# Attention units issued in twos on TensorE, with scores of the two partition halves alternating between two PSUM banks

## The reference, cut to what matters

```
logits = q @ k.T * scale + bias_or_mask      # 128 x nk, nk = 128 for query block 0, 256 for block 1
p      = exp(logits - max(logits)); den = sum(p)
out    = (p @ v) / den * factor              # 128 x 64 (128 x 128 in the differential and memory attention)
```

## Time and profile before

| | |
|---|---|
| median of 3 runs | 1821.94 us |
| lowest, highest | 1797.82, 4195.58 us |
| the profiled execution | 1794.75 us |
| its span, first to last instruction | 1792.9 us |
| PE busy | 94% |
| DVE busy | 60% |
| ACT busy | 47% |
| share of PE in the chain that ended last | 90% |
| mean granted TensorE clock | 0.952 |

### The profile page before, as it was taken

One profiled execution on the slowest core, in us unless ns is written; L12 is line 12 of the kernel. 1 busy time (PEld: TensorE's weight loads), 2 busy tenths in 40 slices (PEclk: granted clock), 3 DMA queues, 4 the chain that ended last, 5 costly groups with the idle time before them and its releaser, 6 DMA issues.

```text
span 1792.9 us, 25005 instructions
## 1 busy us (share of the span) xinstructions
PE 1680.8 (94%) x10388; PEld 1508.4 (84%) x10388; DVE 1069.4 (60%) x1551; ACT 848.0 (47%) x1215; POOL 12.8 (1%) x19
## 2 busy tenths in 40 slices
PE   7969898899998999997979999999999999999998
PEld 7867787799978998785767899879998877789996
DVE  4547566588846554576747655546554775755553
ACT  4446543566535443453336544444443554654441
POOL 0000000000000000000000000000000000000000
PEclk9969999899998999997589999999999999999999
DMA  7723255455553555452034445545555432425553
GB/s 269 274 102 124 78 204 188 142 177 187 188 189 140 188 179 196 166 185 97 1 115 144 159 176 184 188 171 181 188 188 188 165 141 95 159 100 179 177 188 115
DMA packets 42928, 290.21 MB, mean 162 GB/s; under 512 B 5000, under 2 KB 5150, under 8 KB 9920
## 3 DMA queue, kind: packets, MB, share of 16 engines
q1 hardware_dynamic: 38272, 271.93, 42.8%
q0 software_dynamic: 4544, 16.69, 2.8%
HBM read 287.51 MB, written 8.55 MB: 165 GB/s over the span
## 4 chain that ended last, share of the span: by engine, by line
PE 90%; DVE 5%; ACT 2%; DVEq 2%; DMA 1%; issue 1%; SPq 0%; POOL 0%; POOLq 0%; ACTq 0%; PEldq 0%
PE bank L443 26%; PE bank L444 25%; PE bank L445 25%; PE bank L449 8%; PE bank L705 2%; PE bank L1295 2%; DVEq L1990 2%; DVE low L411 1%; DMA raw<-stream_dram 1%; PE bank L595 1%; ACT high L400 0%; PE bank L456 0%; DVE u L924 0%; DVE h L1000 0%; DVE u L648 0%
## 5 line engine op out<-in xcount | busy, mean ns | idle before, releaser
L400 ACT ACTIVATE high<-raw 128x2048 fp32r<-128x2048 f32 x257 | 489.0, 1914 | 560.9 <-DMA raw<-stream_dram 557.8
L411 DVE TENSOR_TENSOR low<-raw,high 128x2048 fp32r<-128x2048 f32 x255 | 581.5, 2289 | 268.5 <-ACT high L400 267.4
L443 PE MATMUL bank<-xh,high 128*128 128x256 f32 x1880 | 535.5, 285 | 1.1 <-DVE low L411 1.1
L444 PE MATMUL bank<-xl,high 128*128 128x256 f32 x1880 | 534.1, 284 | 0.0
L445 PE MATMUL bank<-xh,low 128*128 128x256 f32 x1880 | 534.1, 284 | 0.0
L443 PEld LDWEIGHTS bank<-xh,high 128*128 128x128 f32 x1880 | 363.4, 193 | 2.1 <-issue 2.1
L444 PEld LDWEIGHTS bank<-xl,high 128*128 128x128 f32 x1880 | 363.3, 193 | 0.0
L445 PEld LDWEIGHTS bank<-xh,low 128*128 128x128 f32 x1880 | 363.1, 193 | 0.0
L443 PE MATMUL bank<-high,xh 128*128 128x512 f32 (+2 forms) x528 | 205.0, 388 | 2.2 <-DVE low L411 1.1
L444 PE MATMUL bank<-low,xh 128*128 128x512 f32 (+2 forms) x528 | 203.0, 385 | 0.0
L445 PE MATMUL bank<-high,xl 128*128 128x512 f32 (+2 forms) x528 | 202.8, 384 | 0.0
(11 more groups left out here) (207 smaller groups left out, 1578.5 us busy)
## 6 DMA issues: line engine op xcount, KB each, us to landing
raw<-stream_dram SPq DMA_DIRECT2D x257, 1024.0 KB, 4.8
band_wide_dram<-band_rows_dram POOLq DMA_DIRECT2D x1, 3072.0 KB, 23.0
t_wide_dram<-t_rows_dram POOLq DMA_DIRECT2D x1, 2304.0 KB, 15.3
u<-mem_dram POOLq DMA_DIRECT2D x2, 1024.0 KB, 5.3
bias<-band_wide_dram POOLq DMA_DIRECT2D x1, 2048.0 KB, 9.6
rel_wide_dram<-rel_rows_dram POOLq DMA_DIRECT2D x1, 1920.0 KB, 16.7
bias<-t_wide_dram POOLq DMA_DIRECT2D x1, 1536.0 KB, 7.8
bias<-rel_wide_dram POOLq DMA_DIRECT2D x1, 1280.0 KB, 7.0
```

What stands on the lines that cost most here:

```text
L400: act.activation(self.high[:, n % RING, :], self.raw[:, n % RING, :], ACT.Copy).then_inc(self.high_split, 1)
L411: dve.tensor_tensor(self.low[:, n % RING, :], self.raw[:, n % RING, :], self.high[:, n % RING, :].bitcast(F32), ALU.subtract).then_inc(sel ...
L443: pe.matmul(out, lh, rh, start=start, stop=False)
L444: pe.matmul(out, lh, rl, start=False, stop=False)
```

## The change

PE takes the units in twos. There are four score banks instead of three, `score(i)` issues the scores of units i and i + 1, head by head in turn, each unit into its own bank; `turn` and `value` of two units stand together. ACT runs the exponentials of two units ahead of the two copies. The list of DVE is not touched. The filling matmuls go to bank 4, since bank 7 now holds scores. In `first_units` the loops are exchanged, so that two neighbouring units are on different partition halves. The new lists:

```diff
--- before.py
+++ after.py
@@ -453,7 +453,7 @@
 
 
     for _ in range(n):
-        pe.matmul(core.bank[7][:, 0:S], core.xh[:, 0, 0:P], core.xh[:, 0, :], start=True, stop=True)
+        pe.matmul(core.bank[4][:, 0:S], core.xh[:, 0, 0:P], core.xh[:, 0, :], start=True, stop=True)
 
 
 class Stage:
@@ -1252,6 +1252,7 @@
 class Attention(Stage):
 
 
+
     def __init__(self, core, units, select=None, loads=None, fill=0):
         super().__init__(core)
         self.fill = fill
@@ -1265,24 +1266,26 @@
 
 
 
-    SCORE_BANKS = (0, 1, 6)
+    SCORE_BANKS = (0, 1, 6, 7)
 
     def scores(self, i):
         u = self.units[i]
-        bank = self.core.bank[self.SCORE_BANKS[i % 3]]
+        bank = self.core.bank[self.SCORE_BANKS[i % 4]]
         return bank[:, :].rearrange("p (n k) -> p n k", n=2)[:, 0:u.n, 0:u.nk]
 
     def tensor(self, pe, s):
         c, units = self.core, self.units
 
         def score(i):
-            u = units[i]
-            if i >= 3:
+            two = units[i:i + 2]
+            if i >= 4:
                 pe.wait_ge(s["logits_ready" if units[i - 3].bias is not None else "probs_ready"], i - 2)
-            ps = self.scores(i)
-            for j in range(u.n):
-                last = mm(pe, ps[:, j, :], u.q[j], u.k[j], True, True)
-            last.then_inc(s["scores_ready"], 1)
+            for j in range(2):
+                for n, u in enumerate(two):
+                    if j < u.n:
+                        last = mm(pe, self.scores(i + n)[:, j, :], u.q[j], u.k[j], True, True)
+                        if j == u.n - 1:
+                            last.then_inc(s["scores_ready"], 1)
 
         def turn(i):
             u = units[i]
@@ -1308,15 +1311,17 @@
                               t == 0, t == len(u.parts) - 1)
             last.then_inc(s["out_ready"], 1)
 
-        for i in range(min(3, len(units))):
-            score(i)
+        score(0)
+        score(2)
         keep_clock(pe, c, self.fill)
-        for i in range(len(units) + 1):
+        for i in range(0, len(units) + 2, 2):
             if i < len(units):
                 turn(i)
-            if i + 3 < len(units):
-                score(i + 3)
+                turn(i + 1)
+            if i + 4 < len(units):
+                score(i + 4)
             if i:
+                value(i - 2)
                 value(i - 1)
 
     def scalar(self, act, s):
@@ -1337,9 +1342,11 @@
             last.then_inc(s["probs_ready"], 1)
 
         exp(0)
+        exp(1)
         for i, u in enumerate(units):
-            if i + 1 < len(units):
-                exp(i + 1)
+            if i % 2 == 0 and i + 2 < len(units):
+                exp(i + 2)
+                exp(i + 3)
             act.wait_ge(s["probs_turned"], i + 1)
             if i >= 2:
                 act.wait_ge(s["out_ready"], i - 1)
@@ -1735,20 +1742,19 @@
     for b in range(NB):
         nk, parts = (b + 1) * P, [P] * (b + 1)
         keys, qs = slice(0, nk), block_cut(b)
-        for pair in pairs:
-            q = [half(c.t, h, qs) for h in pair]
-            rows = slice((pair[0] % 2) * DH, (pair[0] % 2 + 1) * DH)
-            heads = slice(pair[0], 4, 2)
-            dst = c.o[:, b, 0:256].rearrange("p (h d) -> p h d", d=DH)[:, heads, :]
-            gates = compress.gates[:, b, :].rearrange("p (h r) -> p h r", r=3)
-            at = 2 * len(units)
-            mask = CONST(c.const, "cmp_mask")[:, 15 * b:15 * b + 15].unsqueeze(1).to_broadcast([P, 2, 15])
-            units.append(Unit(q, [compress.k[rows, 0:15]] * 2, [[compress.v[0:15, :]]] * 2, [15], DH ** -0.5, DH,
-                              scaled(c, dst, compress.cmp_gates[:, b, heads]), slice(at, at + 2), mask))
-
-
-            for r, (kt, v0) in enumerate(((2, 0), (3, DH)), 1):
+        gates = compress.gates[:, b, :].rearrange("p (h r) -> p h r", r=3)
+        mask = CONST(c.const, "cmp_mask")[:, 15 * b:15 * b + 15].unsqueeze(1).to_broadcast([P, 2, 15])
+        for r, (kt, v0) in enumerate(((None, None), (2, 0), (3, DH))):
+            for pair in pairs:
+                q = [half(c.t, h, qs) for h in pair]
+                rows = slice((pair[0] % 2) * DH, (pair[0] % 2 + 1) * DH)
+                heads = slice(pair[0], 4, 2)
+                dst = c.o[:, b, 0:256].rearrange("p (h d) -> p h d", d=DH)[:, heads, :]
                 at = 2 * len(units)
+                if r == 0:
+                    units.append(Unit(q, [compress.k[rows, 0:15]] * 2, [[compress.v[0:15, :]]] * 2, [15], DH ** -0.5, DH,
+                                      scaled(c, dst, compress.cmp_gates[:, b, heads]), slice(at, at + 2), mask))
+                    continue
                 k = c.t[rows, kt, keys]
                 v = [c.u[:, t, v0:v0 + DH] for t in range(b + 1)]
                 units.append(Unit(q, [k, k], [v, v], parts, DH ** -0.5, DH, scaled(c, dst, gates[:, heads, r], add=True),
```

## The result

The changed kernel takes 1870.05 us (median of four runs, 1866.3 to 1874.66); beside it the kernel before took 1821.44 (median). The ratio is 1.039 [1.032, 1.046], slower; its base is some 1800 us, since it leaves the slow executions of the kernel before out, as the ratios of the experiments do, and by the two medians it is 1.027. The profiled execution took 1869.46 us, 74.7 more than the profiled one of before, 1794.75. The gap between 48.6 and 74.7 is a matter of the kernel before, whose runs lie at two levels, near 1795 and near 1820, mostly at the second; the experiment on the kernel before shows why.

What follows compares the result with a forecast made beforehand. PE was taken to set the pace in the attention stages before, a loop over two units after the change. Forecast: 1794.75 + 55 (loop) + 24 (fallen clock) = 1874 us, range 1855 to 1900, eight in ten 1835 to 1905.

Steps and rivals of the forecast that it cites:

- The loop: Attention stages: value(i), finish(i), logits(i+5), exp(i+5), copy(i+2), transposes, scores, value(i+2) close over two units; before, four.
- Its length: One turn, nk = 256, full clock: 3.81 us with PE waiting plus 3.37 us of PE's part, 7.2 against 5.06.
- The sum of 55 us for the loop: Loop's cost by stage: odd 13.4, even 8.5, first 29, memory stages 4 us; good to about +-12.
- The memory term: Memory stages: copies 0 and 1 behind exponentials 2 and 3, copy(2) waiting for value(0); 2 us each, 4 in all.
- The fallen clock: Clock falls during the first and odd stage: 22 us, plus 1 to 3 us behind the odd one; 24 in all.
- The argument for the fall: First and odd stage: PE had no gap, now idles about 3 of 7.2 us, so a clock fall is likely.
- PE's own saving: Paired scores on two halves overlap and need fewer row changes: 7, 13 and some 10 us by stage, 30 in all.
- The engine next in line: Without the loop a pair at nk = 256 could fall from 5.06 to 3.9 us, where PE and DVE meet.
- Loop with a full clock: Rival: the loop binds in the attention stages and the clock holds, 1794.75 + 55 = 1850 us; chance 0.27.
- The loop shorter than added up: Rival: steps overlap, a third to two thirds of the 55 us remain, clock up, 1813 to 1832; chance 0.13.
- PE relieved with nothing in its place: Rival: attention stages faster by up to 30 us, 25 where DVE caps it, 1770 us; chance 0.07.
- No overlap: Rival: halves don't overlap in steady state, 14 us on top of the forecast, 1888 us; chance 0.05, within 0.53.

Runs made afterwards that it cites:

- e1: DVE's list also put in twos (l4 l5 f0 f1), against the changed kernel: 1815.5 us, odd stage 31.68 us.
- e2: PE issues the last pair's values ahead of the next scores, against the changed kernel: 1828.4 us, odd stage 39.65 us.
- e4: ACT's list of before put back, against the changed kernel: 1853.9 us, odd stage 48.49 us.
- e6: 16 filling matmuls a pair added in PE's gap in the first and odd stage, against the changed kernel: 1833.3 us.
- e9: Changed kernel with only scores paired; transposes and values one unit at a time, ACT's list of before: 1777.5 us, ratio 0.975.
- b1: The kernel before, without an edit, profiled once more: 1822.0 us, first stage 76.60 us in place of 46.94.
- e5: e3 with the odd stage's two loops exchanged, so both units of a pair lie on one half: 1806.0 us, odd stage 30.79 us.
- e3: Changed kernel with DVE's list in twos and values ahead of scores on PE: 1798.2 us, ratio 0.997.

## Why the prediction was right, point by point

- **The loop** was right in its members, its order and its cause. The chain goes through the very steps that the prediction named, the waits form the ring DVE, ACT, PE, and undoing any one member shortens it: DVE's list (e1, odd stage 21.9 us shorter), PE's (e2, 13.9), ACT's (e4, 5.1), the first two with what they give back of the clock.
- **Its length** at nk = 256 was put at 3.81 + 3.37 = 7.2 us at full clock; e6 measured 6.81. The part put at 3.81, in which PE waits, is 3.56: among other things, the first copy begins at 1552.53, under the last read of an accumulator, and adds 0.49 us to the chain, not 0.60. From 1 / den to 1 / den two units on, e6's six cycles of the odd stage take 4.98, 4.97, 6.10, 6.81, 5.55 and 5.55 us, against 5.3, 5.3, 6.3, 7.2, 5.9 and 5.9 predicted: 34.0 in all against 35.9.
- **The sum of 55 us for the loop** was too large: e6 shows 22.3 in the first stage (predicted 29), 11.2 in the odd one (13.4) and 3.4 for the memory stages together (4). The even stage cost 3.4, not 8.5, and this is the worst of the terms by share: 40 us in all. (By its own terms PE's part of an even cycle is 5.96 us, not 5.9, which changes nothing.) In the even stage the prediction kept the clock at 0.50 as in the earlier trace rows; in fact it rises in pulses between the gaps, 0.61 in the mean, and that can pay for a part of the longer loop; how much was not measured by itself. In the reckoning of e6 its filling matmuls count as free. In the odd stage they are; in the first one what they cost is in the 22.3, so the loop may be a little cheaper still. The memory term had the right size, but taking away the exponentials ahead of the copies, to which it was put down in part, does not bring the time back (e4, 8.1 us); single turns and values do (e9, 6.3).
- **The fallen clock** was too small: 34 us (21.3 + 12.8) in place of the 22 for the two stages. It fell at 146.5 us, 6.6 us into the first stage and not after three or four cycles, and in the odd stage was low for most of 1522 to 1573. The 1 to 3 us behind the odd stage are not shown: that stretch is 2.8 us longer, but in e6, whose clock did not fall, it is 2.0 us longer as well. The two errors, -15 in the loop and +12 in the clock, largely cancel: 74 us in the five stages against 77, and 1870 against 1874. That the forecast is so near is in part luck.
- **The argument for the fall** was only half of it. Gaps go with a fallen clock, and filling them keeps it at 1.00 (e6). But "PE used to have no gap, so the clock held" is not the cause: b1 has no gap and falls. The prediction's baseline was the rarer kind of execution; against the usual 1821 the change costs 49 us, and 1874 came near the measured time because the changed kernel falls to the low clock anyway.
- **PE's own saving** was right, and hidden. The overlap was predicted at 0.87 us a pair at nk = 256 and is 0.86 (e5 against e3). Predicted in all: 30 us. e9, which has the saving without the loop, is 29.0 us below 1794.75: 5.2, 14.0 and 6.1 in the first, even and odd stage (predicted 10, 13, 7), 0.4 in the memory stages and some 3 elsewhere. The nearness of 29.0 to 30 is partly luck: the first stage gives half of what was predicted, the 3 us elsewhere are no part of the saving, and the even stage's 14.0 include a clock of 0.78 in place of 0.50.
- **The engine next in line.** The prediction held that PE and DVE would meet at 3.9 us a pair. e9's pair takes 3.83. DVE's share was put too high, though: its units follow each other every 1.72 us there, not 1.9 (1 / den at 1457.66, 1459.37, 1461.09 and 1462.80), 3.4 a pair. Both engines are all but full: from 1452 to 1467 us PE has a matmul in flight in 14.58 of 15 us, and DVE is busy in 14.22 and never waits for more than 0.1 us. The Trainium skill, page "TensorEngine Tiling", section "PSUM Bottleneck", says that after a fourfold speedup of TensorE the copy out of PSUM may become the bottleneck; here a saving of 1.2 us in 5.06 was enough to fill DVE, though no experiment shows which of the two engines limits e9.
- **The rivals.** Loop with a full clock, 1850: built as e6, it gave 1833. The loop shorter than added up, 1813 to 1832 with the clock up: true of the loop in part, since 40 of the 55 us remain (e6), but the clock fell. PE relieved with nothing in its place, 1770: wrong for this change, and nearly the time of e9, which is what it would have taken. No overlap: excluded by e5.
- **The rest**: that the projections keep their length to 1 us holds for their sum (0.3 us), not for each stretch between the attention stages (-3.6 to +2.8 us). Part of that is no effect of the change: b1 has -5.7 to +1.4 us against the first profile of the same kernel.

## What to carry to other kernels

Before an engine's list is regrouped, write down the in-order lists of the others and close every ring through them: here values that come one pair later on PE met a list of DVE that wants them before the next logits, the ring closed over two units in place of four, and 6.8 us a pair (9.45 with the clock fallen) took the place of 5. Take the part of a change that saves work (two units' scores, on two halves and in two banks) apart from the rest (turns, values and exponentials in twos): with the kernel before at 1820 us, the first alone takes 1777 here, both together 1870. And profile the kernel before more than once, since a single profile may be of its rarer level.

## What the runs showed of the hardware

- The granted clock can fall under a PE that always has a matmul in flight: b1, from 1.00 at 138 to 142 us to 0.50 behind 146, with PE busy in 4.00 of 4.00 us each time. The Trainium skill, page "TensorE: Matmul & The Clock Gate", section "What's actually happening", has the gate follow how busy the array has been; by busy time in the profile's sense b1 should have kept its clock, and it did not. What differs between the two kinds of execution of the same program stays open.
- The reverse too: the clock can rise in pulses under a PE with gaps. The changed kernel's even stage has a mean of 0.61 with PE busy in 40.86 of 60 us, and e9's 0.78 with PE busy in 32.57 of 43, against 0.50 in the earlier trace rows with PE busy in 57.80 of 60. That the gaps are the reason is not shown.
- Two 64-row score blocks on different halves and in different banks cost no more than one: 8 records in 1.13 us (e3), as 4 records in the earlier trace rows, against 1.99 on one half (e5). In both the two blocks lie in different banks, so what the banks do by themselves is not shown.
- Two copies directly behind an exponential take 1.06 us together, not twice 0.60, and the first starts at 1552.53, before the last accumulator read (1552.44 to 1552.63) has ended.
